# The expert layer's head, last job and tail rewritten: routing on unscaled logits, a last job of its own, returned rows summed on VectorE, a final norm per token tile

## The chip, the cores and the metric

The kernel runs on one core of a Trainium2 chip. The metric is the device time of one execution in microseconds (us), the median of several runs. The program is written instruction by instruction: each engine (PE = TensorE, ACT = ScalarE, DVE = VectorE, POOL = GpSimd, SP = SyncE) has its own list, carried out in order, and semaphores are the only coupling between lists.

## The reference, cut to what matters

Two blocks of two layers each run on 256 tokens of width 1024 in fp32. The change touches the last layer's expert feed-forward and the final norm:

```python
def rmsnorm(x, g, eps): return x * rsqrt(mean(x * x) + eps) * g
h = rmsnorm(x, ffn_norm_g[1])
logits = h @ router                          # 8 experts
top_v, top_i = lax.top_k(logits, 2)
top_w = softmax(top_v)
out = 0
for e in range(8):                           # w1, w3: 1024 x 3584, w2: 3584 x 1024
    gate_e = sum(where(top_i == e, top_w, 0))
    out = out + gate_e * ((silu(h @ w1[e]) * (h @ w3[e])) @ w2[e])
x = x + out
return rmsnorm(x, final_norm_g)
```

## The kernel before

**Weights.** Every weight passes through the core once, in chunks of 128 x 2048 fp32 (1 MB), in the order of use. SP loads them into a ring `raw` of RAW = 6 tiles and waits on `w_used` for a free one (`fetch`, L655 to L659). ACT rounds each chunk to `hi` (ring of HI = 3, `conv`, L1286 is ACT's one helper line), DVE writes the rest `lo = raw - hi` over `raw` (`conv`, L1685), and PE multiplies activations, split likewise, by both: three matmuls (hi·hi, lo·hi, hi·lo) where one fp32 product is meant, 12 of 512 columns for a chunk.

**Expert layer.** Tokens are sorted to experts on the chip. A job is one expert with up to 128 tokens; jobs 0 to 7 are the experts, and up to MORE = 3 further jobs take an expert's tokens beyond 128. In the profiled run there are 8 jobs, 0 to 7. A job has J = 14 blocks of 256 hidden units, each of three chunks: two for w1 and w3 (`up`, L1204 to L1206) and one for w2 (`down_rows`, L1185 to L1187). `job_walk` is the order that all engines share: in the turn of block j come `u0(j+1)` (first chunk of the next block), `tr(j)` (PE transposes `gprod`, ACT writes `ghi`, DVE `glo`, L2208), `u1(j+1)` (second chunk; then ACT's silu and DVE's `gprod`, L2204), and `dn(j)`. At each of the three chunk steps ACT and DVE convert the chunk two ahead. A job's `dn(13)` is done after the next job's `u0(0)`. `late` (in the turn of block 12) transposes the next job's token rows `xg` and splits them into `xhi`, `xlo`; `behind` (after `u1(0)`) evacuates the job before into `y`, and in job 0 runs DVE's `job_tables`. Ten of the blocks are two bodies in an inner hardware loop; jobs 1 to 7 are one outer hardware loop (`each_job`), with a second one under an `If` for the further jobs.

**Head.** The norm's transposed columns come as four pairs of `xhi`/`xlo` tiles. PE waits for all four, then forms the router's logits (24 matmuls, L1251 to L1253); DVE copies them (`lgT`), PE transposes, DVE multiplies by 1/rms (`lg8`), finds the two best experts, writes `chosen`; PE ranks the tokens by expert (L1263 to L1266); DVE makes the gates and then, from the rank, the one-hot `pick`. `gather` (L1153) multiplies the normalised rows `hrow` by `pick`, which gives job 0's columns. DVE goes on with the tokens' places, up to `where_i`, and splits the gathered columns (`gathered`).

**Other jobs' rows.** POOL writes the normalised rows to DRAM, fetches each next job's slots and rows (`fetch_rows`), and stores each finished job's `y` to `expert_rows` (512 KB). After the job loop it gathers, by four indirect DMAs of 512 KB, the rows that each token has in `expert_rows` (`back`), multiplies them by their shares (L2489, four of 128 x 1024), and adds them into `x` (L2492, L2493), all during job 7.

**Tail.** Job 7 fetches rows and one weight chunk for a job 8 that doesn't exist, and converts that chunk. Then PE does the last `dn(13)`, transposes `pick_g`, and four matmuls (`scatter`, L1172) return job 7's rows to their tokens; DVE adds them to `x` (L2196). The final norm squares both token tiles, takes Ln and Exp for 1/rms of both, and DVE scales (L1707); SP stores each tile.

## Time and profile before

| | |
|---|---|
| median of 3 runs | 2585.55 us (2585.35 to 2586.4) |
| the profiled execution | 2585.76 us |
| its span, first to last instruction | 2583.9 us |
| PE busy | 2509.5 us (97%) |
| DVE, ACT, POOL busy | 1818.7, 1521.9, 183.6 us |
| expert layer in the span | about 1577 to 2584 us |

A row of the timeline gives start, duration, engine, line, operation, output and inputs; a bracket holds the idle time before it and what ended it. "x8" means that many instructions in one row. PE's matmuls overlap: a 128 x 512 one is shown as 0.39 us long, yet they start every 0.23 us. The profile lists a weight load and a matmul for each; an fp32 (not rounded) matmul shows as two of each.

### The profile page before, as it was taken

The numbers are of one execution on the slowest core, as the hardware profiler recorded it, in microseconds if no ns is written. First come the engines' busy times: TensorE is split into PE (matmuls) and PEld (weight loads), VectorE is DVE, ScalarE is ACT, GpSimd is POOL, SyncE is SP. The second block draws the span as 40 slices with busy tenths as digits, with TensorE's granted clock in tenths as the row PEclk, the third lists the DMA queues.
The fourth block names the chain that finished last, engine by engine and source line by source line (L and its number), as shares of the span: only waits on it lengthen the run. The fifth ranks groups of instructions, "written<-read, shape, count | busy, mean of one in ns | idle before, by whom it ended". The sixth has DMA issues, their size and how long they took to land.

```text
span 2583.9 us, 32235 instructions
## 1 busy us (share of the span) xinstructions
PE 2509.5 (97%) x11900; PEld 2068.5 (80%) x11900; DVE 1818.7 (70%) x1795; ACT 1521.9 (59%) x1581; POOL 183.6 (7%) x141
## 2 busy tenths in 40 slices
PE   6999999999999999999999998999999999999997
PEld 5888788788878878878888876888888888888876
DVE  5577754557775555665555467888888888888887
ACT  5455544454544354545445555777777777777766
POOL 0100200010020000020000012000000000000060
PEclk8999999999999999999999999999999999999999
DMA  6444455444445564545554455999999999999995
GB/s 220 147 147 163 166 192 183 161 160 151 163 163 187 187 205 151 180 164 179 193 181 161 163 179 206 364 370 383 380 377 374 376 385 376 383 368 386 373 361 224
DMA packets 90564, 635.24 MB, mean 246 GB/s; under 512 B 10477, under 2 KB 10853, under 8 KB 15472
## 3 DMA queue, kind: packets, MB, share of 16 engines
q1 hardware_dynamic: 85104, 617.41, 65.0%
q0 software_dynamic: 4896, 16.09, 1.8%
q8 instruction: 56, 0.92, 0.1%
q10 hardware_dynamic: 480, 0.59, 0.1%
q14 instruction: 28, 0.23, 0.0%
HBM read 626.57 MB, written 7.48 MB: 245 GB/s over the span
## 4 chain that ended last, share of the span: by engine, by line
PE 88%; DVE 4%; ACT 3%; issue 3%; DMA 1%; DVEq 0%; SPq 0%; ACTq 0%
PE bank L716 13%; PE bank L718 12%; PE bank L717 12%; PE bank L1206 7%; PE bank L1204 7%; PE bank L1205 7%; PE bank L1185 4%; PE bank L1187 4%; PE bank L1186 4%; PE bank L731 3%; PE bank L733 3%; PE bank L732 3%; PE bank L705 3%; DVE w_lo L1685 2%; ACT w_hi L1286 1%
## 5 line engine op out<-in xcount | busy, mean ns | idle before, releaser
L1685 DVE TENSOR_TENSOR w_lo<-raw,w_hi 128x2048 fp32r<-128x2048 f32 x586 | 1359.2, 2322 | 492.5 <-ACT w_hi L1286 480.0
L1286 ACT ACTIVATE w_hi<-raw 128x2048 fp32r<-128x2048 f32 x586 | 1121.6, 1915 | 269.2 <-PE bank L733 102.1
L716 PE MATMUL bank<-w_hi,xhi 128*128 128x512 f32 x1456 | 580.4, 399 | 13.2 <-DVE w_lo L1685 7.5
L718 PE MATMUL bank<-w_lo,xhi 128*128 128x512 f32 x1456 | 569.7, 391 | 0.0
L717 PE MATMUL bank<-w_hi,xlo 128*128 128x512 f32 x1456 | 569.4, 391 | 0.0
L1204 PE MATMUL bank<-w_hi,xhi 128*128 128x512 f32 x896 | 359.0, 401 | 2.4 <-DVE w_lo L1685 2.4
L1206 PE MATMUL bank<-w_lo,xhi 128*128 128x512 f32 x896 | 350.2, 391 | 0.0
L1205 PE MATMUL bank<-w_hi,xlo 128*128 128x512 f32 x896 | 349.5, 390 | 0.0
L716 PEld LDWEIGHTS bank<-w_hi,xhi 128*128 128x128 f32 x1456 | 274.9, 189 | 71.8 <-issue 12.5
L718 PEld LDWEIGHTS bank<-w_lo,xhi 128*128 128x128 f32 x1456 | 274.6, 189 | 58.9
L717 PEld LDWEIGHTS bank<-w_hi,xlo 128*128 128x128 f32 x1456 | 275.2, 189 | 54.0
L1206 PEld LDWEIGHTS bank<-w_lo,xhi 128*128 128x128 f32 x896 | 168.2, 188 | 35.7
L1204 PEld LDWEIGHTS bank<-w_hi,xhi 128*128 128x128 f32 x896 | 168.3, 188 | 35.3 <-DVE w_lo L1685 3.9
L1286 ACT ACTIVATE ghi<-bank 128x256 fp32r<-128x256 f32 x178 | 64.8, 383 | 219.2 <-PE bank L705 219.2
L1205 PEld LDWEIGHTS bank<-w_hi,xlo 128*128 128x128 f32 x896 | 168.7, 188 | 31.6
L1185 PE MATMUL bank<-w_hi,ghi 128*128 128x512 f32 x448 | 176.9, 395 | 10.7 <-DVE glo L2208 10.7
L1186 PE MATMUL bank<-w_hi,glo 128*128 128x512 f32 x448 | 175.1, 391 | 0.0
L1187 PE MATMUL bank<-w_lo,ghi 128*128 128x512 f32 x448 | 175.1, 391 | 0.0
L2447 POOL TENSOR_TENSOR u<-u,gates 128x512 f32<-128x512 f32 x32 | 61.1, 1938 | 705.6 <-DVE gates L2091 705.6
L1185 PEld LDWEIGHTS bank<-w_hi,ghi 128*128 128x128 f32 x448 | 84.5, 189 | 32.5 <-DVE w_lo L1685 12.3
L731 PE MATMUL bank<-w_hi,ghi 128*128 128x512 f32 x264 | 103.0, 390 | 3.3 <-DVE glo L2152 3.3
L733 PE MATMUL bank<-w_lo,ghi 128*128 128x512 f32 x264 | 102.8, 389 | 0.0
(364 smaller groups left out, 2462.8 us busy)
## 6 DMA issues: line engine op xcount, KB each, us to landing
raw<-in_wexpert SPq DMA_DIRECT2D x337, 1024.0 KB, 5.1
raw<-in_wdense SPq DMA_DIRECT2D x249, 1024.0 KB, 4.8
expert_rows<-y POOLq DMA_DIRECT2D x7, 512.0 KB, 4.5
expert_rows<-back POOLq DMA_DIRECT2D x3, 512.0 KB, 3.8
x<-in_x SPq DMA_DIRECT2D x2, 512.0 KB, 4.9
biasT<-bias_rows POOLq DMA_DIRECT2D x1, 1024.0 KB, 6.7
normal_rows<-hrow POOLq DMA_DIRECT2D x1, 1024.0 KB, 6.3
out<-hrow SPq DMA_DIRECT2D x2, 512.0 KB, 2.7
```

The lines of the kernel that those rows point to most:

```text
L716: mm(bank[banks[t]][:, :], xhi[:, k0 + k, tok], wh, start=start and k == 0, stop=False)
L717: mm(bank[banks[t]][:, :], xlo[:, k0 + k, tok], wh, start=False, stop=False)
L718: last = mm(bank[banks[t]][:, :], xhi[:, k0 + k, tok], wl, start=False, stop=stop and k == 3)
L731: mm(b, xh, hi[:, h, o:o + 512], start=first and k == 0, stop=False)
L1185: mm(dst, ghi[:, m, 0, :], hi[:, h, w], start=first, stop=False)
L1186: mm(dst, glo[:, m, 0, :], hi[:, h, w], start=False, stop=False)
L1187: last = mm(dst, ghi[:, m, 0, :], lo[:, s, w], start=False, stop=final)
L1204: mm(bank[b][:, :], xhi[:, kt, 0:P], hi[:, h, w], start=kt == 0, stop=False)
L1205: mm(bank[b][:, :], xlo[:, kt, 0:P], hi[:, h, w], start=False, stop=False)
L1206: last = mm(bank[b][:, :], xhi[:, kt, 0:P], lo[:, s, w], start=False, stop=kt == KT - 1)
L1286: return nc.scalar.activation(dst, src, f, **kw)
L1685: V.tensor_tensor(lo[:, c % RAW, :], raw[:, c % RAW, :], hi[:, c % HI, :].bitcast(F32), ALU.subtract).then_inc(lo_ready, 1)
```

## The change

In the head the router's matmuls wait pair by pair; the experts are chosen on the logits before the 1/rms scaling, and only the difference of the two best is scaled; `rank` and `pick` come before the gates; `pick` carries 1/rms, so that `gather` reads the rows with gain alone and the normalised rows go to a tile `hnorm`; `rows_i` is written later, and half of `gathered` comes earlier. `job_tables` is split: the table for the returned rows stays, the further jobs' tables follow one by one after blocks 0 to 2 and the list after block 3. Job 0 and the last job are written out without the inner loop, and the last job is called apart from the loops. In it nothing is fetched for a next job; DVE adds the returned rows in eight 128 x 512 steps after blocks 4 to 11; `ghi`/`glo` alternate between two tiles, and the last block's transposes lie between the halves of `dn(12)`; `dn(13)` goes by output half, with `pick_g`'s transposes between. The final norm takes Square, Sqrt, a reciprocal and the scaling for each token tile, with one Sqrt ahead.

```diff
     tr(0, 0)
     u1(1, 0, 4)
     dn(0, 0, 5)
+    after(0)
+    n = 0 if first or last else (J - 3) // 2
+    if n:
+        with eng.Fori(0, n) as it:
...
     for j in range(1 + 2 * n, J - 1):
         u0(j + 1, 0, 3 + 3 * j)
         tr(j, 0)
         u1(j + 1, 0, 4 + 3 * j)
-        if j == J - 2:
+        if j == J - 2 and not last:
             late()
         dn(j, 0, 5 + 3 * j)
+        after(j)
     tr(J - 1, 0)
 def each_job(eng, job):
-    job(0, True)
+    job(0, True, False)
     eng.wait_ge(routed, 1)
     nj = eng.value_load(jobs_i[0:1, MORE + 1:MORE + 2], min_val=NE, max_val=NE + MORE)
-    with eng.Fori(1, NE) as e:
-        job(e, False)
+    end = eng.value_load(jobs_i[0:1, MORE + 2:MORE + 3], min_val=NE - 1, max_val=NE + MORE - 1)
+    with eng.Fori(1, NE - 1) as e:
+        job(e, False, False)
     with eng.If(nj > NE):
-        with eng.Fori(NE, nj) as e:
-            job(e, False)
+        with eng.Fori(NE - 1, end) as e:
+            job(e, False, False)
+    job(end, False, True)
     return nj
...
     fetch(c0 - 1, chunk(before, per - 1), nj, per)
-    fetch(c0, a["wexpert"][0, 0], nj, per)
     for t in range(NT):
-        sp.wait_ge(norm_h, NT * len([k for k in phases if k[0] == "moe"]) + t + 1)
+        sp.wait_ge(norm_h, t + 1)
         sp.dma_start(out[t * P:t * P + P, :], hrow[:, t, :]).then_inc(stored, 16)
     sp.wait_ge(stored, 16 * NT)
...
+        def turned():
+            b = X[2]
+            pe.wait_ge(pick_ready, 2)
+            pe.wait_ge(free[b], use((k, "turned"), b))
+            for t in range(NT):
+                done = tr(bank[b][:, t * P:t * P + P], pick_g[:, t, :])
+            done.then_inc(full[b], 1)
+        down_rows(k, J, J - 1, 0, 0, nj, between=turned, by_half=True)
         for b, (t, n) in zip((X[2], X[3], 2, 3), ((0, 0), (0, 1), (1, 0), (1, 1))):
             pe.wait_ge(free[b], use((k, "scatter"), b) + JU[b] * last)
+            pe.wait_ge(free[X[n]], ev((k, "D"), X[n]) + JU[X[n]] * last)
             mm(bank[b][:, :], pick_t[:, t, :], y[:, n * 512:n * 512 + 512], start=True, stop=True).then_inc(full[b], 1)
-    def down_rows(k, J, j, it, o, e, job=None):
+    def down_rows(k, J, j, it, o, e, job=None, between=lambda: None, by_half=False):
...
+        def part(m, n):
+            dst, first, final = bank[X[n]][:, :], j == 0 and m == 0, j == J - 1 and m == 1
+            w = slice(m * 1024 + n * 512, m * 1024 + n * 512 + 512)
+            mm(dst, ghi[:, m, j % 2, :], hi[:, h, w], start=first, stop=False)
+            mm(dst, glo[:, m, j % 2, :], hi[:, h, w], start=False, stop=False)
+            return mm(dst, ghi[:, m, j % 2, :], lo[:, s, w], start=False, stop=final)
+        for i in range(2):
+            for r in range(2):
+                last = part(r, i) if by_half else part(i, r)
+            if i == 0:
+                if by_half:
+                    last.then_inc(half_done, 1)
+                between()
         last.then_inc(w_used, 1)
...
         def turn(j, it):
             b = j % 2
+            if last and j == J - 1:
+                return
+            turn_block(j, it)
+        def turn_block(j, it):
+            b = j % 2
...
+            down_rows(k, J, j, it, c, e, None if j == J - 1 else e,
+                      between=(lambda: turn_block(J - 1, 0)) if last and j == J - 2 else lambda: None)
...
             b = X[0]
-            for i in range(4):
-                pe.wait_ge(free[X[i]], ev(("norm", k[1], "moe"), X[i]))
             pe.wait_ge(router_split, 1)
             for kt in range(KT):
+                if kt % 2 == 0:
+                    pe.wait_ge(free[X[kt // 2]], ev(("norm", k[1], "moe"), X[kt // 2]))
                 o = bank[b][0:NE, 0:S]
...
-    def rows_done(k, J, o, e):
-        act.wait_ge(w_used, CH[k] - 1 + o + 1 + 3 * J * e)
+    def rows_done(k, J, o, e, by_half=False):
         for n in range(2):
+            if by_half and n == 0:
+                act.wait_ge(half_done, HALF[k, "last"])
+            else:
+                act.wait_ge(w_used, CH[k] - 1 + o + 1 + 3 * J * e)
             go(y[:, n * 512:n * 512 + 512], bank[X[n]][:, :], ACT.Copy).then_inc(free[X[n]], 1)
...
             def normalised(t):
                 act.wait_ge(rows_gained, t + 1)
-                go(hrow[:, t, :], hrow[:, t, :], ACT.Copy, scale=nstat[:, 4 + t:5 + t]).then_inc(norm_h, 1)
+                go(hnorm[:, t, :], hrow[:, t, :], ACT.Copy, scale=nstat[:, 4 + t:5 + t]).then_inc(rows_normal, 1)
             normalised(0)
...
-            for t in range(NT):
-                last = go(top2[:, t, 0:1], m8[:, t, 1:2], ACT.Exp, bias=top2[:, t, 1:2])
-            last.then_inc(route_e, 1)
+            go(top2[:, :, 0:1], top2[:, :, 1:2], ACT.Exp).then_inc(route_e, 1)
             normalised(1)
             gathered(k, 0)
-            rows_done(k, FFJ["moe"], 0, nj)
-            def last_job(t):
+            rows_done(k, FFJ["moe"], 0, nj, True)
+            link(go(nstat[:, 6:7], nstat[:, 4:5], ACT.Sqrt))
+            for t in range(NT):
                 for b in ((X[2], X[3]), (2, 3))[t]:
                     act.wait_ge(free[b], ev((k, "scatter"), b) + JU[b] * (nj - 1))
-            norm(("norm", 0, None), n, None, last_job)
+                link(go(hrow[:, t, :], x[:, t, :], ACT.Square, accum_out=nstat[:, t:t + 1]))
+                go(nstat[:, 4 + t:5 + t], nstat[:, t:t + 1], ACT.Sqrt, scale=1.0 / D, bias=eps1).then_inc(root_ready, 1)
...
         if f is None:
-            dve.wait_ge(norm_rstd, n + 1)
+            moe = phases[-1][0] == "moe"
+            if not moe:
+                dve.wait_ge(norm_rstd, n + 1)
             dve.wait_ge(fgain_in, 16)
             for t in range(NT):
+                if moe:
+                    dve.wait_ge(root_ready, t + 1)
+                    link(V.reciprocal(nstat[:, 4 + t:5 + t], nstat[:, 4 + t:5 + t]))
                 V.scalar_tensor_tensor(out=hrow[:, t, :], in0=x[:, t, :], scalar=nstat[:, 4 + t:5 + t], in1=fgain[:, :],
                                        op0=ALU.mult, op1=ALU.mult).then_inc(norm_h, 1)
...
     def pick_first():
         for t in range(NT):
-            last = V.tensor_scalar(pick[:, t, :], C("slots"), jobpos[:, t, 0:1], None, ALU.is_equal)
+            last = V.tensor_scalar(pick[:, t, :], C("slots"), jobpos[:, t, 0:1], nstat[:, 4 + t:5 + t], ALU.is_equal, ALU.mult)
         last.then_inc(pick_ready, 1)
...
     def scattered(k, e):
-        dve.wait_ge(x_summed, NT)
+        dve.wait_ge(x_summed, 4 * NT)
...
+    def returned(p):
+        t, i, n = p // 4, p // 2 % 2, slice(p % 2 * 512, p % 2 * 512 + 512)
+        if p == 0:
+            dve.wait_ge(rows_back, 16 * 2 * NT)
+        dve.wait_ge(x_summed, p)
+        V.scalar_tensor_tensor(out=x[:, t, n], in0=back[i][:, t, n], scalar=share_w[:, t, i:i + 1], in1=x[:, t, n],
+                               op0=ALU.mult, op1=ALU.add).then_inc(x_summed, 1)
+    def expert_job(k, J, e, first, last):
+        def down(j, it, c):
+            if not (last and j == J - 2):
+                conv(c0 + c + 2, it, e, per)
+        def after(j):
+            if first and j < 1 + MORE:
+                if j < MORE:
+                    further_job(j)
+                else:
+                    job_list()
+            if last and 4 <= j < 4 + 4 * NT:
+                returned(j - 4)
         def up_done(j, it, c):
-            conv(c0 + c + 2, it, e, per)
+            n = c0 + c + 2
+            if last and j == J - 1:
+                dve.wait_ge(hi_ready, n + 1 + per * e)
+                halves = [(lo[:, n % RAW, w], raw[:, n % RAW, w], hi[:, n % HI, w].bitcast(F32)) for w in (slice(0, 1024), slice(1024, 2048))]
+                V.tensor_tensor(*halves[0], ALU.subtract)
+            else:
+                conv(n, it, e, per)
...
             V.tensor_tensor(gprod[:, 0, :], bank[j % 2][:, FB:2 * FB], silu[:, 0, :], ALU.mult).then_inc(free[j % 2], 1)
+            if last and j == J - 1:
+                V.tensor_tensor(*halves[1], ALU.subtract).then_inc(lo_ready, 1)
...
     def route(k):
-        V.tensor_copy(rows_i[:, :, :], C("tokens").unsqueeze(2).to_broadcast([P, NT, 16]))
...
-        dve.wait_ge(norm_rstd, len([p for p in phases if p[0] == "norm"]))
-        V.tensor_tensor(lg8[:, :, :], two(bank[b][:, 0:16]), nstat[:, 4:6].unsqueeze(2).to_broadcast([P, NT, NE]),
-                        ALU.mult).then_inc(free[b], 1)
+        V.tensor_copy(lg8[:, :, :], two(bank[b][:, 0:16])).then_inc(free[b], 1)
...
-            V.max_index(i8[:, t, :], m8[:, t, :], lg8[:, t, :])
-            last = V.tensor_scalar(top2[:, t, 1:2], m8[:, t, 0:1], -1.0, None, ALU.mult)
-        last.then_inc(route_m, 1)
-        dve.wait_ge(route_m, 1)
+            last = V.max_index(i8[:, t, :], m8[:, t, :], lg8[:, t, :])
+        link(last)
...
         last.then_inc(chosen_ready, 1)
+        dve.wait_ge(norm_rstd, len([p for p in phases if p[0] == "norm"]))
+        link(V.tensor_tensor(top2[:, :, 1:2], m8[:, :, 1:2], m8[:, :, 0:1], ALU.subtract))
+        V.tensor_tensor(top2[:, :, 1:2], top2[:, :, 1:2], nstat[:, 4:6].unsqueeze(2), ALU.mult).then_inc(route_m, 1)
+        dve.wait_ge(chosen_ready, 1)
+        b, key = X[1], (k, "rank")
+        wait_full(key, b)
+        V.tensor_copy(rank[:, :, :].rearrange("p t n -> p (t n)"), bank[b][:, 0:24]).then_inc(free[b], 1)
+        dve.wait_ge(free[b], ev(key, b))
+        link(V.scalar_tensor_tensor(out=rank[:, 0:NT, :], in0=chosen[:, :, :], scalar=1e6, in1=rank[:, 0:NT, :],
+                                    op0=ALU.mult, op1=ALU.add))
+        link(V.tensor_scalar(jobpos[:, :, 0:NE], rank[:, 0:NT, :], 1000001.0, None, ALU.subtract))
+        pick_first()
         dve.wait_ge(route_e, 1)
...
+        gathered(k, 0, (0,))
...
+        V.tensor_copy(rows_i[:, :, :], C("tokens").unsqueeze(2).to_broadcast([P, NT, 16]))
         V.tensor_copy(where_i[:, :, :], where_f[:, :, :]).then_inc(places_ready, 1)
-        gathered(k, 0)
-    def job_tables():
+        gathered(k, 0, (1,))
+    def return_tables():
...
+        V.tensor_scalar_add(jobs_f[:, MORE + 2:MORE + 3], jobs_f[:, MORE + 1:MORE + 2], -1.0)
...
-        V.tensor_copy(back_i[:, :, :], back_f[:, :, :])
-        for i in range(MORE):
+        link(V.tensor_copy(back_i[:, :, :], back_f[:, :, :]))
+    def further_job(i):
+        link(V.tensor_scalar(over[:, 3, :], over[:, 1, :], over[:, 2, i:i + 1], None, ALU.is_equal))
+        link(V.tensor_tensor(prod8[:, :, :], jobtab[:, :, 0:NE], over[:, 3, :].unsqueeze(1).to_broadcast([P, 2 * NT, NE]),
+                             ALU.mult))
...
     def expert_jobs(k):
...
-        pool.wait_ge(norm_h, NT)
-        pool.dma_start(normal_rows.rearrange("(t p) d -> p t d", p=P), hrow[:, :, :]).then_inc(normal_out, 16)
+        pool.wait_ge(rows_normal, NT)
+        pool.dma_start(normal_rows.rearrange("(t p) d -> p t d", p=P), hnorm[:, :, :]).then_inc(normal_out, 16)
...
-        def job(e, first):
+        def job(e, first, last):
             if not first:
...
                 pool.dma_start(expert_rows[bass.ds((e - 1) * P, P), :], y[:, :]).then_inc(y_out, 16)
                 pool.wait_ge(y_out, 16 * e)
-                for b in (2, 3):
-                    pool.wait_ge(full[b], fl((k, "next"), b) + JF[b] * (e - 1))
                 pool.wait_ge(pulsed, e)
-            fetch_rows(e + 1)
+            if last:
+                G.tensor_tensor(pulse[:, 1:2], pulse[:, 0:1], pulse[:, 0:1], ALU.add).then_inc(pulsed, 1)
+            else:
+                if not first:
+                    for b in (2, 3):
+                        pool.wait_ge(full[b], fl((k, "next"), b) + JF[b] * (e - 1))
+                fetch_rows(e + 1)
...
-        pool.wait_ge(rows_back, 16 * 2 * NT)
-        for t in range(NT):
-            for i in range(2):
-                last = G.tensor_scalar(back[i][:, t, :], back[i][:, t, :], share_w[:, t, i:i + 1], None, ALU.mult)
-        link(last)
-        for t in range(NT):
-            link(G.tensor_tensor(back[0][:, t, :], back[0][:, t, :], back[1][:, t, :], ALU.add))
-            G.tensor_tensor(x[:, t, :], x[:, t, :], back[0][:, t, :], ALU.add).then_inc(x_summed, 1)
```

## Rows read from the trace of the kernel before

**Rows 1.** The page's busy time of each engine.
```profile
PE 2509.5 (97%) x11900; PEld 2068.5 (80%) x11900; DVE 1818.7 (70%) x1795; ACT 1521.9 (59%) x1581; POOL 183.6 (7%) x141
```

**Rows 2.** Windows: stretch, length, busy PE, PEld, DVE, ACT, POOL; clock, DMA share, GB/s.
```profile
500.00:1000.00 500.00, 492.95 (x2436) 410.04 (x2437) 304.99 (x349) 253.60 (x307) 36.17 (x29) 1.00 0.51 172
...
1620.00:1720.00 100.00, 100.00 (x456) 82.19 (x455) 89.52 (x62) 74.79 (x62) 0.00 (x0) 1.00 0.97 370
...
2465.20:2485.30 20.10, 17.87 (x77) 13.55 (x75) 14.91 (x11) 12.84 (x11) 7.84 (x3) 1.00 1.02 422
2485.30:2525.30 40.00, 36.38 (x153) 28.97 (x153) 38.95 (x21) 24.92 (x19) 26.27 (x7) 0.96 0.86 336
```

**Rows 3.** Timeline of DVE and PE, one block of a job in the steady stretch.
```profile
1652.15 2.29 DVE L1685 TENSOR_TENSOR w_lo<-raw,w_hi 128x2048 fp32r<-128x2048 f32 x1 [0.15 <-ACT w_hi L1286]
...
1655.36 2.29 DVE L1685 TENSOR_TENSOR w_lo<-raw,w_hi 128x2048 fp32r<-128x2048 f32 x1 [0.58 <-ACT w_hi L1286]
...
1655.71 0.39 PE L1185 MATMUL bank<-w_hi,ghi 128*128 128x512 f32 x1
...
1660.59 2.29 DVE L1685 TENSOR_TENSOR w_lo<-raw,w_hi 128x2048 fp32r<-128x2048 f32 x1 [0.15 <-ACT w_hi L1286]
```

**Rows 4.** Timeline of DVE and PE in the head.
```profile
1579.72 3.23 DVE L1695 SCALAR_TENSOR_TENSOR xlo<-bank,par,xhi 128x256 fp32r<-128x256 f32 x8 [0.28 <-ACT xhi L1286]
...
1583.21 0.28 PE L1251 MATMUL bank<-xhi,router_hi 128*8 128x256 f32 x1 [2.73 <-DVE xlo L1695]
...
1587.62 0.41 DVE L2221 COPY lgT<-bank 8x256 f32<-8x256 f32 x1 [2.21 <-PE bank L1253]
...
1590.53 0.36 PE L1263 MATMUL bank<-chosen,cst 128*128 128x8 f32 x2 [2.16 <-DVE chosen L2240]
...
1592.29 0.18 DVE L2255 COPY rank<-bank 128x24 f32<-128x24 f32 x1 [0.17 <-PE bank L1266]
...
1593.51 5.94 PE L1153 MATMUL bank<-pick,hrow 128*128 128x128 f32 x32 [1.26 <-issue]
```

**Rows 5.** Waits of PE, 1577 to 1616 us: in total, times, longest.
```profile
PE bank L1185 <- DVE glo L2208: 2.8, 1, 2.8
```

**Rows 6.** Timeline of DVE in job 0, around `job_tables`.
```profile
1607.57 0.17 DVE L2297 CAST back_i<-back_f 128x4 int32<-128x4 f32 x1
...
1610.48 2.34 DVE L1685 TENSOR_TENSOR w_lo<-raw,w_hi 128x2048 fp32r<-128x2048 f32 x1
```

**Rows 7.** Timeline of PE: the first matmul of `dn(2)`, `dn(4)` and `dn(8)` in job 7.
```profile
2465.21 0.39 PE L1185 MATMUL bank<-w_hi,ghi 128*128 128x512 f32 x1
...
2485.34 0.49 PE L1185 MATMUL bank<-w_hi,ghi 128*128 128x512 f32 x1 [1.15 <-DVE glo L2208]
...
2525.30 0.39 PE L1185 MATMUL bank<-w_hi,ghi 128*128 128x512 f32 x1
```

**Rows 8.** Waits of ACT, 2465 to 2486 us.
```profile
ACT w_hi L1286 <- DMA raw<-in_wexpert: 5.4, 5, 1.9
```

**Rows 9.** Timeline of PE and DVE in the tail.
```profile
2558.93 1.03 PE L705 MATMUL bank<-ident_t,xg 128*128 128x128 f32 x8
...
2562.49 2.29 DVE L1685 TENSOR_TENSOR w_lo<-raw,w_hi 128x2048 fp32r<-128x2048 f32 x1
...
2565.24 0.49 PE L1185 MATMUL bank<-w_hi,ghi 128*128 128x512 f32 x1 [2.32 <-DVE glo L2208]
...
2569.43 3.70 PE L1172 MATMUL bank<-y,pick_t 128*128 128x512 f32 x8 [0.96 <-ACT y L1286]
...
2573.17 0.69 DVE L2196 TENSOR_TENSOR x<-bank,x 128x512 f32<-128x512 f32 x1 [0.17 <-PE bank L1172]
```

**Rows 10.** Timeline of ACT and DVE in the final norm.
```profile
2575.12 1.28 ACT L1286 ACT_TABLE_LOAD   x1
...
2578.26 2.48 DVE L1707 SCALAR_TENSOR_TENSOR hrow<-x,nstat,fgain 128x1024 f32<-128x1024 f32 x2 [4.40 <-ACT nstat L1286]
```

**Rows 11.** DMA queues, 500 to 1000 us: packets, MB, share of the 16 engines.
```profile
q8 instruction: 17, 0.28, 0.2%
```

96 lines of the change are left out of this document (35 added, 61 removed).

## The prediction

> **What bounds the kernel now.** I read the page's busy times first: PE is busy for 97% of the span [rows 1], so only time in which PE stands still, or does something that the change removes, can be won. The windows show the steady part of a job: PE has no idle time, the DMA engines are at 0.97, and DVE is busy for 89.5 of 100 us [rows 2]. One block takes 1660.59 - 1652.15 = 8.44 us, the distance between the same conversion in two blocks [rows 3]. That is 36 matmuls at one per 0.23 us and two transposes, so PE sets the pace, and DVE has 10.5% of 8.44 = 0.88 us free in a block. Three views give what is not steady: the timeline of the head [rows 4], of the first block of job 0 [rows 5, 6], of job 7 [rows 2, 7, 8], and the tail [rows 9, 10]. All edits lie there; jobs 1 to 6 keep their code but for the choice of a `ghi` tile.
>
> **The head: 3.7 us.** The router starts only when all four pairs are split, at 1583.21, and its 24 matmuls last until the copy `lgT` at 1587.62, 4.41 us [rows 4]. Waited for in pairs, six matmuls follow each pair of `xlo`; DVE makes the eight tiles in 3.23 us, 0.81 a pair, so only the last six matmuls remain after 1583.21. A quarter of 4.41 is 1.1; the first ones are faster than the mean (0.28 us long, less than half of which is their distance), so I take 0.85, and `lgT` starts at about 1584.05: 3.55 us won. If TensorE's clock falls earlier than before, they take up to 1.3 and 3.1 is won. `rows_i`'s cast and the wait for 1/rms leave the path. From `lgT` to `chosen` two of the small steps go (L2232, each under 0.15, partly overlapped): 0.15. PE's rank matmuls then take 1590.53 to 1592.29 as before, and DVE was waiting for them [rows 4], so the gates that move behind `pick` (eight small instructions) were hidden there and gain nothing by their move. Where do they go? In front of the gathered columns' split: after `pick` DVE has eight steps of the gates and nine of the shifts, at about 0.2 us each 3.4 us, against half of 5.94 us and ACT's rounding, 3.6 us, until the first half can be split; so they are covered. `gather` is 5.94 us as before. First half split, then places, then second half: PE needs the second half only after `u0(0)`, 2.8 us later. The two steps for the difference of the logits fall into DVE's wait for the rank. `gather` starts 3.55 + 0.15 = 3.7 us earlier. Bounds: 2.5 and 4.2.
>
> **Job 0: 2.8 us.** PE waits once for 2.8 us in `dn(0)` for `glo` [rows 5], because `job_tables` holds DVE until 1610.48 with the conversion behind it [rows 6]. The part that stays ends with `back_i` at 1607.74 plus one hidden addition, so the conversion starts 2.7 us earlier and `glo` as well; PE's wait goes. The other tables return as 0.7 us after each of blocks 0 to 3, below the 0.88 us free. Bounds: 2.0 and 2.8.
>
> **POOL's sums in job 7: 6.2 us.** From `dn(4)` at 2485.34 to `dn(8)` at 2525.30 four blocks took 39.96 us where 4 x 8.44 = 33.76 are due [rows 7]. In that stretch POOL is busy for 26 us (L2489 to L2493) and DVE for 38.95 of 40.0 us with only the usual work [rows 2]: DVE's conversions read two tiles in SBUF and get slower while POOL works there. DVE is what PE waits for. The sums leave POOL, so 6.2 us come back. What takes their place is eight DVE steps of 128 x 512 with a scalar and a tensor. The nearest row is the same operation at 128 x 1024, two in 2.48 us [rows 10]: 0.62 us each and a little fixed cost, 0.67. One per block, below 0.88 us. It comes right after `dn`'s conversion; the next conversion starts 0.5 us late, `glo` too, and the pause of 0.58 us before the second conversion [rows 3] takes it up. `glo` ended at 1655.36 - 0.58 = 1654.78 and PE first wanted it at 1655.71 [rows 3], so that cover holds with 0.4 us to spare; without it each step costs up to 0.67, 5.4 in all. I take 0.3 for the two tight places together (here and job 0).
>
> **The gather's traffic: 0.5 us.** Just before, from `dn(2)` to `dn(4)`, two blocks took 20.13 us instead of 16.88, 3.25 us lost [rows 7], with ACT waiting for weight chunks for 5.4 us [rows 8] and the DMA engines at 1.02 and 422 GB/s, against 370 in the steady part [rows 2]. The four gathers (2 MB) stay. What goes is the fetch of 512 KB of rows for a job that doesn't exist, and the gathers start some 6 us earlier, close behind `y`'s 512 KB. So the same 2.5 MB come in one lump rather than 3 MB with a pause. I take 0.5; bounds -0.5 and 3.2.
>
> **The tail: 8.0 us.** The eight transposes of `xg` that start at 2558.93 [rows 9] go, and `dn(12)` starts in their place. Half of it is six matmuls, 1.4 us, in which `gprod` gets ready, since DVE converts half a chunk (1.15 us) before it and not a whole one. Transposes 0.3, second half 1.4: `dn(13)` can start at 2558.93 + 3.05 = 2562.0, while `ghi` (0.4) and `glo` (0.4) are made. Before, `glo` stood behind the conversion of a chunk that nobody uses (2562.49 to 2564.78), and PE waited 2.32 us, to 2565.24 [rows 9]. That is 3.25 us. `dn(13)` with `pick_g`'s transposes lasts 2.86 + 0.3, to 2565.1, and the first half of `y` is evacuated meanwhile: the return matmuls start at 2565.15 instead of 2569.43, 4.3 us earlier [rows 9]. Their last addition starts 2573.17 - 4.3 = 2568.9 and ends at 2569.6. Then, for the second token tile: Square with its accumulator 1.2, Sqrt 0.3, reciprocal 0.2, scaling 1.24, with 0.1 for links: 2572.7. Before, the second scaling ended at 2578.26 + 2.48 = 2580.7, behind two table loads of 1.28 us and the squares and scalings of both tiles in one row [rows 10]. The store behind it is the same 512 KB. 8.0 us in all. The Sqrt ahead needs a table load and 0.3: from 2565.7 (second half of `y`) to 2567.3, in front of the first Square at 2567.9. That Square brings no load of its own is open: behind `y`'s copy it brought none. If it does, two loads more per tile, 2.6 us. Bounds of the tail: 5.4 and 8.5.
>
> The Trainium skill, "ScalarE: Activation LUTs", section "Table sets: the hidden batching unit", gives about 2.7 us for one table load. By it the Sqrt ahead would end at about 2568.7, after the first Square is due, and the tail would give an estimated 0 to 0.8 us less; this trace has 1.28 us, so I go by the row.
>
> **Code outside the loops.** The last job is reached by a branch over the unused `If` and by one more register load, where the jobs before follow each other in a loop. No row shows that branch; PE has at most about what it waited after leaving the loop at the end, 2.32 us [rows 9], and that wait has `glo` as its cause. I take 0.5, bounds 0 and 2.3. The tail is then reached without a branch, where it was hidden anyway.
>
> **Sum.** 3.7 + 2.8 + 6.2 + 0.5 + 8.0 - 0.3 - 0.5 = 20.4 us. Against the profiled execution's own 2585.76 us: 2565.4. The median of the runs is 0.2 us lower: 2565.2. I call 0.2% (5.2 us) the least that tells from no change.
>
> **The rivals.**
> - *DVE becomes the bound in job 0 and the last job.* For: only 0.2 us of its free time is left in such a block, and PE's use of `glo` is close. Against: the rows' pauses add up. If half of each inserted step shows, 8 x 0.33 + 4 x 0.35 = 4.0 us: 2569.
> - *The gather's stall goes altogether*, since the ring has recovered and less is fetched: 2.8 us more, 2562.4. Against: 422 GB/s was the ceiling, and 2 MB at it are 5 us of the weights' time.
> - *The branch to the last job is exposed on PE:* 1.8 us more than I charge, 2567. The Trainium skill, "Runtime: NRT & Kernel Launch", section "Instruction fetch mechanics", says that a taken branch whose target isn't in the fetched pages waits for a DMA of code. No run here shows it yet.
> - *Slower: the written-out jobs wait for their code.* Jobs 0 and 7 lose their inner loop, and code pages then come through DMA engines that are at 0.97. In the straight code from 500 to 1000 us 17 such pages were fetched [rows 11], one per 29 us, so two jobs of 118 us need about eight. From 20.4 / 8 = 2.6 us of PE time per page on, the change loses; at 3.5 us it gives 2593. Against: in that straight part PE was idle for only 7 us in all, under 0.5 a page, though with the DMA engines at 0.51 [rows 2].
> - *It doesn't do what it says:* if POOL's work was not what slowed DVE, but the DMA traffic, the 6.2 us stay: 2571.4. Against: DMA share is 0.86 in that stretch [rows 2].
>
> **How the numbers follow.** Forecast (2563.5 to 2567.5): 0.56. DVE the bound: 0.14. No stall: 0.10. Branch: 0.10. The sums' 6.2 us stay: 0.04. Slower: 0.03. Anything that leaves it within 0.2%: 0.03. Two in ten out leaves 2562 to 2571, which takes in the no-stall case and the upper ones but a Square load together with them. Faster by over 0.2%: 0.95, within: 0.02, slower: 0.03.
>
> **What would show it.** `gather` starts about 3.7 us earlier than 1593.51; no wait over 0.5 us at `dn(0)` of job 0; DVE's conversions stay at 2.29 us through the last job, with one step of 0.67 us per block and blocks of 8.44 us; PE waits under 0.3 us between `dn(12)` and `dn(13)`; the table load before the first Square, none after; the span ends about 11 us after `dn(13)`'s last matmul. The prediction is wrong if Squares bring loads, if blocks 4 to 11 of the last job are longer than 8.6 us, or if PE stands still for over 1 us before the last job.

## The result, and the profile after

The changed kernel takes 2569.41 us (median of 4 runs, 2568.81 to 2570.49), the kernel before 2585.86 us beside it (2585.35 to 2586.4). The ratio is 0.9938, 95% interval 0.9926 to 0.9951: 16.5 us faster. The forecast was 2565.2 us, so it is 4.2 us too low. The result lies inside the wide range (2562 to 2571) and outside the 2563.5 to 2567.5 us to which the forecast gave 0.56. The profiled execution took 2570.49 us; its span is 2568.9 us, 15.0 less than the 2583.9 of before. Where do they come from? I cut both spans at TensorE's transposes: those of the expert layer's norm, the last ones of job 6, and those of blocks 0 and 12 of the last job. The rows of this and later groups are of the timeline: start, length, engine, line, operation.

TensorE after the change, the transposes that cut the span (L708) and what the head starts:

```profile
1577.66 1.06 PE L708 MATMUL bank<-ident_t,x 128*128 128x128 f32 x8 [0.20 <-issue]
1580.22 0.28 PE L1270 MATMUL bank<-xhi,router_hi 128*8 128x256 f32 x1 [0.27 <-DVE xlo L1716]
1588.89 6.71 PE L1156 MATMUL bank<-pick,hrow 128*128 128x128 f32 x32 [1.45 <-issue]
1595.36 0.48 PE L1216 MATMUL bank<-w_hi,xhi 128*128 128x512 f32 x1
...
2427.74 0.38 PE L708 MATMUL bank<-ident_t,gprod 128*128 128x128 f32 x2
2445.90 0.38 PE L708 MATMUL bank<-ident_t,gprod 128*128 128x128 f32 x2
...
2549.38 0.38 PE L708 MATMUL bank<-ident_t,gprod 128*128 128x128 f32 x2
```

The same of the kernel before:

```profile
1578.18 1.06 PE L705 MATMUL bank<-ident_t,x 128*128 128x128 f32 x8 [0.20 <-issue]
...
2433.70 0.38 PE L705 MATMUL bank<-ident_t,gprod 128*128 128x128 f32 x2
2444.83 0.38 PE L705 MATMUL bank<-ident_t,gprod 128*128 128x128 f32 x2
...
2555.97 0.38 PE L705 MATMUL bank<-ident_t,gprod 128*128 128x128 f32 x2
```

| stretch | before | after | difference |
|---|---|---|---|
| up to the norm (code not changed) | 1578.18 | 1577.66 | -0.52 |
| norm to the end of job 6 (head, job 0) | 855.52 | 850.08 | -5.44 |
| job 6 to block 0 of the last job | 11.13 | 18.16 | **+7.03** |
| blocks 0 to 12 of the last job | 111.14 | 103.48 | -7.66 |
| from there to the end of the span | 27.93 | 19.52 | -8.41 |

Four stretches give 22.0 us, 21.5 of it in changed code, close to the forecast's 20.9 of gains, and one takes 7.0 back. That one is the surprise. What does TensorE do there? Its rows in the changed kernel, at the step from the loop over jobs to the last job:

```profile
2432.06 0.79 PE L1216 MATMUL bank<-w_hi,xhi 128*128 128x512 f32 x1 [3.94 <-issue]
...
2437.34 0.63 PE L1189 MATMUL bank<-w_hi,ghi 128*128 128x512 f32 x1
...
2438.15 0.40 PE L1191 MATMUL bank<-w_lo,ghi 128*128 128x512 f32 x1
```

The windows, among them that step, with the columns of [rows 2]:

```profile
1588.80:1596.00 7.20, 7.11 (x35) 7.06 (x36) 5.23 (x30) 1.28 (x3) 0.72 (x1) 0.57 0.96 328
1596.00:1620.00 24.00, 23.92 (x108) 19.37 (x107) 21.77 (x23) 19.74 (x16) 9.33 (x7) 1.00 0.85 324
...
2430.00:2436.00 6.00, 3.94 (x9) 3.15 (x10) 2.60 (x2) 0.83 (x1) 0.00 (x0) 0.60 0.43 169
2482.00:2550.00 68.00, 68.00 (x310) 56.09 (x309) 65.28 (x49) 50.70 (x41) 0.00 (x0) 1.00 0.93 357
```

TensorE stands still for 3.94 us, and "issue" says that no semaphore held it. Between 2430 and 2436 us the granted clock is 0.60, and the matmuls come one per 0.43 us: that is the lower level, 1.2 GHz, where 0.23 us is the upper one. The 14 from 2432.06 to 2438.15 take 6.1 us where 3.2 are due. 3.9 of pause and 2.9 of slow matmuls are 6.8 of the 7.0 us. The other windows answer to [rows 2, 5]: no wait of 2.8 us in job 0, TensorE busy without a gap in blocks 4 to 12 of the last job.

The tail after the change:

```profile
2552.34 0.39 PE L1189 MATMUL bank<-w_hi,ghi 128*128 128x512 f32 x1
...
2555.31 0.40 PE L1189 MATMUL bank<-w_hi,ghi 128*128 128x512 f32 x1
...
2558.32 3.69 PE L1177 MATMUL bank<-y,pick_t 128*128 128x512 f32 x8
...
2559.13 1.28 ACT L1305 ACT_TABLE_LOAD   x1
```

One step of the returned rows on VectorE, in block 6:

```profile
2504.32 2.29 DVE L1706 TENSOR_TENSOR w_lo<-raw,w_hi 128x2048 fp32r<-128x2048 f32 x1
2506.53 0.75 DVE L2230 SCALAR_TENSOR_TENSOR x<-back,share_w,x 128x512 f32<-128x512 f32 x1
2507.19 2.29 DVE L1706 TENSOR_TENSOR w_lo<-raw,w_hi 128x2048 fp32r<-128x2048 f32 x1
```

The step takes 0.75 us and the conversions on both sides keep their 2.29. In the tail, `dn(12)` starts at 2552.34 and `dn(13)` 2.97 us later, without the wait of [rows 9]; the returning products begin at 2558.32; the table load lies before the first Square and none follows it.

### The profile page after: what moved, and what is told of

Read it like the earlier page. It is cut to its first block, busy times and chain, and to the rows that moved or that the text cites. A ratio compares the mean times of both kernels' runs of the same rounds, so it can differ in the third digit from the quotient of the medians.

```text
span 2568.9 us, 32012 instructions
## 1 busy us (share of the span) xinstructions
PE 2509.1 (98%) x11892; PEld 2069.5 (81%) x11892; DVE 1807.3 (70%) x1804; ACT 1520.3 (59%) x1576; POOL 153.2 (6%) x131
## 4 chain that ended last, share of the span: by engine, by line
PE 91%; ACT 3%; DVE 3%; issue 2%; DMA 1%; SPq 0%; ACTq 0%; DVEq 0%
PE bank L719 13%; PE bank L721 12%; PE bank L720 12%; PE bank L1216 7%; PE bank L1218 7%; PE bank L1217 7%; PE bank L1189 4%; PE bank L1191 4%; PE bank L1190 4%; PE bank L708 3%; PE bank L734 3%; PE bank L736 3%; PE bank L735 3%; ACT w_hi L1305 1%; PE bank L1095 1%
## 5 line engine op out<-in xcount | busy, mean ns | idle before, releaser
L1706 DVE TENSOR_TENSOR w_lo<-raw,w_hi 128x2048 fp32r<-128x2048 f32 x584 | 1343.3, 2302 | 494.7 <-ACT w_hi L1305 482.5
```

Source lines behind the costliest of these rows:

```text
L1706: V.tensor_tensor(lo[:, c % RAW, :], raw[:, c % RAW, :], hi[:, c % HI, :].bitcast(F32), ALU.subtract).then_inc(lo_ready, 1)
```

## The experiments

Single times of one kernel lay up to 5.7 us apart (e3b_pool_sums), and the transposes of the norm, ahead of which no experiment changes code, start anywhere from 1576.11 (the short If) to 1579.45 us (tables in one piece) in the profiled runs. So each experiment is read twice: by its median and by a distance inside its trace. "Distance" below is that from the last transposes of the loop's last job to the first ones of the last job (11.13 before, 18.16 after). The runs of before beside them had medians of 2585.88 to 2586.06 us.

**e1_no_if and e2_one_loop: what pauses TensorE.** In `each_job`, e1 only leaves the If out; e2 makes one loop of both:

```
-            with eng.Fori(1, NE - 1) as e:
+            with eng.Fori(1, end) as e:
                 job(e, False, False)
-            with eng.If(nj > NE):
-                with eng.Fori(NE - 1, end) as e:
-                    job(e, False, False)
             job(end, False, True)
```

> The changed kernel with the unused If (the loop over further jobs) left out on TensorE, VectorE, ScalarE and GpSimd, so that the code of the last job follows the loop's end directly; the case of more than eight jobs is thereby left out. In the changed kernel 18.2 us pass on TensorE between the last transposes of the loop's last job and the first ones of the last job, where the kernel before took 11.13 us. Theory A (the branch over the If leaves the code that is fetched in sequence): the pause of 3.9 us and the slow matmuls behind it go, the distance falls to 11.5 us or less and the time to 2562.5 us (2561.5 to 2564). Rival B (any exit from the loop into code not run before waits for its fetch): the distance stays at 16 to 18 us and the time at 2569. Rival C (the low clock has another cause than the pause): the pause goes and the slow matmuls stay, 2565.

> The changed kernel with the fixed loop over jobs 1 to 6 and the If joined into one loop that ends at the register's value, so that no branch lies between it and the last job and further jobs are still served. Theory A: like the kernel without the If, 2562.5 us (2561.5 to 2564), distance from the last transposes of the loop to the first of the last job 11.5 us or less. Rival B: 2569 and 16 to 18 us. Rival D (a loop whose end is in a register costs at each turn): 0.3 us or more longer at each of the six job boundaries than the kernel without the If.

Measured: 2564.31 us (2561.62 to 2565.66), ratio 0.9914 [0.9898, 0.9931], and 2564.14 us (2562.3 to 2565.06), 0.9915 [0.9899, 0.9932]. The distance is 11.13 us in both. TensorE of the one-loop kernel at the step:

```profile
2427.64 0.38 PE L705 MATMUL bank<-ident_t,gprod 128*128 128x128 f32 x2
2427.77 0.48 PE L1213 MATMUL bank<-w_hi,xhi 128*128 128x512 f32 x1
...
2438.77 0.38 PE L705 MATMUL bank<-ident_t,gprod 128*128 128x128 f32 x2
```

The pause and the slow matmuls go together, and leaving a loop for code that was never run costs nothing by itself (B falls). C falls too: without the pause the clock keeps its upper level. A loop end in a register costs nothing against a fixed one (D falls). The medians fell by 5.1 and 5.3 us, less than the 7.0 of the distance and at the upper edge of what I gave or just beyond. The other kernels with the branch had distances of 16.27 (e3_pool_sums) and 16.21 us (e8_no_returned), so the branch costs 5 to 7 us, differently from run to run. Both of its parts are shorter in these two. TensorE stands still for 3.30 and 3.22 us, and the matmuls behind it reach the upper level after about 8, not 14. The first matmul behind the branch, in e3_pool_sums and in e8_no_returned:

```profile
2430.05 0.79 PE L1216 MATMUL bank<-w_hi,xhi 128*128 128x512 f32 x1 [3.30 <-issue]
...
2430.11 0.67 PE L1216 MATMUL bank<-w_hi,xhi 128*128 128x512 f32 x1 [3.22 <-issue]
```

So the medians, with 5.1 and 5.3 us, fit the branch as these two traces show it better than they fit the 7.0 us of the changed kernel's profiled execution, which was also the slowest of its four.

**e9_short_if: a branch, or a far branch.**

```
             with eng.If(nj > NE):
-                with eng.Fori(NE - 1, end) as e:
-                    job(e, False, False)
+                eng.value_load(jobs_i[0:1, MORE + 1:MORE + 2], ...)
```

> The changed kernel with the If still there and evaluated, but with one register load as its body in place of the loop over further jobs, which is thereby left out. Measured so far: 18.2 us between the last transposes of the loop's jobs and the first of the last job in the changed kernel, 11.13 us where no If lies between. Theory A1 (what costs is how far the branch jumps, past code that was fetched): 11.1 to 12 us here and a time within 1 us of the one-loop kernel's, 2564 us. Rival (evaluating the If and taking any branch costs): 15 to 18 us here and 2568 to 2570 us.

Measured: 2562.32 us (2561.3 to 2565.76), ratio 0.991 [0.9893, 0.9927], distance 2436.77 - 2425.63 = 11.14 us. The If and its branch cost nothing when one register load is jumped over, and 5 to 7 us when it is the code of a whole job; lengths between these two weren't run. The median is 0.8 us further off than I allowed, on the good side. Code pages fetched between 2428 and 2430 us and between 2430 and 2434 us in the changed kernel (queue: packets, MB, share):

```profile
q8 instruction: 1, 0.02, 2.9%
...
q8 instruction: 1, 0.02, 1.7%
q14 instruction: 1, 0.01, 0.5%
```

The one-loop kernel and this one have no such row between 2420 and 2440 us. The kernel before takes the same branch once, behind job 7, and two pages of the same queue come there as well. Its code pages between 2562 and 2567 us, then the windows of TensorE's pause in it and in the changed kernel:

```profile
q8 instruction: 2, 0.03, 3.0%
...
2562.92:2565.24 2.32, 0.01 (x1) 0.00 (x1) 2.32 (x3) 0.38 (x1) 0.00 (x0) 1.00 0.01 4
...
2428.12:2432.06 3.94, 0.00 (x1) 0.01 (x1) 3.38 (x3) 2.30 (x2) 0.00 (x0) 0.90 0.95 331
```

There TensorE resumes within 0.2 us of the end of `glo` (2564.69 us, 0.42 long), so the branch was over by then: it took at most 2.32 us, and the matmuls behind it came at the upper level, one per 0.23 us. The DMA engines' share was 0.01 in that pause. It was 0.95 in the pause of 3.94 us, 0.83 in that of 3.30 and 0.76 in that of 3.22. The pause is longer the busier the DMA engines are, in four traces; no run changes the traffic alone, so this cause is not shown. The Trainium skill's rule ("Runtime: NRT & Kernel Launch", "Instruction fetch mechanics"), that a taken branch to a target outside the fetched pages stalls for a DMA, agrees with all of these runs.

**e10_if_but_pe: whose code.**

```
-        def each_job(eng, job):
+        def each_job(eng, job, joined=False):
...
+            if joined:
+                with eng.Fori(1, end) as e:
+                    job(e, False, False)
+            else:
+                with eng.Fori(1, NE - 1) as e:
+                    job(e, False, False)
+                with eng.If(nj > NE):
+                    with eng.Fori(NE - 1, end) as e:
+                        job(e, False, False)
```

TensorE's call has `joined` true, the others' not.

> The changed kernel with one loop over the jobs on TensorE's own program and the loop with the If behind it on VectorE, ScalarE and GpSimd. Theory A2 (it is TensorE's own program that waits for code): the distance between those transposes falls to below 12.5 us and the time to 2564 us. Rival (the other engines' branches hold the conversions back, and TensorE would wait for them as soon as its own wait goes): a wait for w_lo or glo of 2 us or more shows on TensorE at the start of the last job, and the distance stays at 14 us or more.

Measured: 2563.53 us (2562.93 to 2564.62), ratio 0.991 [0.9894, 0.9927], distance 2439.74 - 2428.57 = 11.17 us. TensorE's own program is what waits. Between 2420 and 2440 us the rows of q8 are gone too, although the other three engines still jump, and only one page of q14 is left. The two pages of q8 come with TensorE's jump. ScalarE, which still jumps, shows a pause of its own there, and it is hidden:

```profile
2429.75 3.91 ACT L1309 ACTIVATE w_hi<-raw 128x2048 fp32r<-128x2048 f32 x2 [0.38 <-issue]
```

**e3_pool_sums and e3b_pool_sums: the sums back on GpSimd,** on the changed kernel and on the one-loop kernel.

```
-                    if last and 4 <= j < 4 + 4 * NT:
-                        returned(j - 4)
...
+                pool.wait_ge(rows_back, 16 * 2 * NT)
+                for t in range(NT):
+                    for i in range(2):
+                        last = G.tensor_scalar(back[i][:, t, :], back[i][:, t, :], share_w[:, t, i:i + 1], None, ALU.mult)
+                link(last)
+                for t in range(NT):
+                    link(G.tensor_tensor(back[0][:, t, :], back[0][:, t, :], back[1][:, t, :], ALU.add))
+                    G.tensor_tensor(x[:, t, :], x[:, t, :], back[0][:, t, :], ALU.add).then_inc(x_summed, 1)
...
+                        act.wait_ge(rows_back, 16 * 2 * NT)
```

> The changed kernel with the sums of the returned rows back on GpSimd, as in the kernel before, and none on VectorE; ScalarE waits for the returned rows before the last evacuation. Theory (VectorE's reads of two tiles slow down while GpSimd works): blocks 4 to 8 of the last job take 6 us longer in all, conversions there 3 to 4 us instead of 2.29, time 2575.5 us (2574.5 to 2577). Rival (it was the traffic, which stays as it is here): blocks stay at 8.41 us, time 2569.

> The one-loop kernel with the sums of the returned rows on GpSimd, none on VectorE. On the changed kernel this edit gave 13.44 us for block 5, 9.42 for block 6 and 6.2 us in all, but only 3.9 us in the medians, with the branch's pause differing by 1.9 us between the profiled runs. Theory (the sums cost 6 us and the medians differ by the pause's and the start's variation): 6 us more than the one-loop kernel, 2570 us (2569 to 2571.5). Rival (the profile exaggerates, 3.9 us is the true price): 2568 us.

Measured: 2573.26 us (2572.15 to 2574.79), ratio 0.9953 [0.9936, 0.9969], 3.9 over the changed kernel; and 2572.28 us (2568.12 to 2573.83), 0.9942 [0.9925, 0.9958], 8.1 over the one-loop kernel. The medians miss both of my figures, one on each side; their mean is 6.0. The traces agree with each other. Transposes of blocks 4, 5, 6, 7 and 8 in e3b_pool_sums, and its VectorE meanwhile:

```profile
2476.94 0.38 PE L705 MATMUL bank<-ident_t,gprod 128*128 128x128 f32 x2
2485.49 0.38 PE L705 MATMUL bank<-ident_t,gprod 128*128 128x128 f32 x2
2498.54 0.38 PE L705 MATMUL bank<-ident_t,gprod 128*128 128x128 f32 x2
2508.38 0.38 PE L705 MATMUL bank<-ident_t,gprod 128*128 128x128 f32 x2
2516.80 0.38 PE L705 MATMUL bank<-ident_t,gprod 128*128 128x128 f32 x2
```

```profile
2482.62 8.59 DVE L1704 TENSOR_TENSOR w_lo<-raw,w_hi 128x2048 fp32r<-128x2048 f32 x2
...
2491.46 4.14 DVE L1704 TENSOR_TENSOR w_lo<-raw,w_hi 128x2048 fp32r<-128x2048 f32 x1
```

Four blocks take 39.86 us, where the changed kernel takes 33.63 (from 2482.13 to 2515.76): 6.2 us, the term of the forecast. In e3_pool_sums they take 2518.41 - 2478.55 = 39.86 as well. Two conversions of the fence take 4.3 us each and one 4.14, instead of 2.29, at a DMA share of 0.75 from 2484 to 2508 us. In the changed kernel the share is 1.00 in blocks 4 to 8 and they keep 2.29. So it isn't the traffic.

Which part of GpSimd's work does it? GpSimd multiplies until 2481.96 us and then adds, in four steps until 2497.88. From e3b_pool_sums, the multiplications, two conversions beside them, and the first addition:

```profile
2466.40 15.56 POOL L2550 TENSOR_SCALAR back<-back,share_w 128x1024 f32<-128x1024 f32 x4 [11.68 <-DMA back<-expert_rows,back_i]
...
2474.24 5.07 DVE L1704 TENSOR_TENSOR w_lo<-raw,w_hi 128x2048 fp32r<-128x2048 f32 x2
...
2482.04 2.59 POOL L2553 TENSOR_TENSOR back<-back,back 128x1024 f32<-128x1024 f32 x1
```

Beside the multiplications, which read one tile, a conversion takes 2.3 to 2.9 us; beside the additions, which read two, 4.1 to 4.3. Most of the price is that of the additions. No run moves only one of the two.

The cut at block 4 hides a part. The multiplications begin before it, and blocks 2 to 8 as a whole take 2516.80 - 2457.39 = 59.41 us in e3b_pool_sums against 52.06 in the one-loop kernel, 7.35 us more; for e3_pool_sums against the changed kernel it is 58.36 against 52.44, 5.92 us more. This is one reason why the medians lie so far apart.

**e8_no_returned: the gathers' traffic.** The four indirect gathers, `returned` and the wait for it are left out.

> The changed kernel without the four gathers of the returned rows and without their sums, so the output leaves out what jobs 0 to 6 return. Theory (their 2 MB beside the weights' stream cost the one long block, 10.39 us instead of 8.41): all blocks of the last job take 8.41 us and the time falls by 2.0 us, to 2567.4 us. Rival (the stream is behind already, since the stretch of 18 us at the job's start moved only 227 GB/s and the fetch of rows follows): the long block stays, 2569. If the VectorE steps cost something too, which the blocks of 8.40 to 8.42 us say they don't, the time falls by more than 2.5 us.

Measured: 2567.16 us (2564.66 to 2569.15), ratio 0.993 [0.9913, 0.9947], 2.25 us below the changed kernel. The median can't be put down to the gathers alone, because the branch's distance also differs between the two traces (16.21 and 18.16 us). The blocks can be compared. Blocks 2 to 4 take 2476.93 - 2460.12 = 16.81 us there; in the changed kernel the block from 2471.74 to 2482.13 alone is 2.0 us too long. Blocks 4 to 8 take 33.63 us in both, so VectorE's eight steps cost nothing. The output of this run leaves out what jobs 0 to 6 return.

**e11_spread: the same gathers, apart.** On the one-loop kernel:

```
+                        if g:
+                            pool.wait_ge(rows_back, 16 * g)
+                            pool.wait_ge(lo_ready, CH[k] + 6 + 6 * g + 3 * FFJ["moe"] * (nj - 1))
+                            G.tensor_tensor(pulse[:, 2:3], pulse[:, 0:1], pulse[:, 0:1], ALU.add).then_inc(paced, 1)
+                            pool.wait_ge(paced, g)
...
-                if p == 0:
-                    dve.wait_ge(rows_back, 16 * 2 * NT)
+                if p % 2 == 0:
+                    dve.wait_ge(rows_back, 16 * (p // 2 + 1))
```

> The one-loop kernel with the four gathers of the returned rows issued apart: each waits for the one before and for a weight chunk two blocks further on, and each VectorE step pair waits for its own gather. Measured so far: one long block, 10.2 us for 8.41, in the one-loop kernel and none without the gathers. Theory (2 MB in one lump hold the weights' stream up for longer than it is ahead; 0.5 MB at a time it can bear): the long block goes, 1.7 us less than the one-loop kernel's 2564.1 us: 2562.4 us. Rival (the stream has no slack at all at a DMA share of 0.97 in the steady part, so each gather of 1.25 us at 420 GB/s shows later as a wait of TensorE): four blocks longer by 0.4 us or more each, time 2564 us or more.

Measured: 2561.44 us (2560.76 to 2562.18), ratio 0.9903 [0.9887, 0.992], 2.7 us below the one-loop kernel and 8.0 below the changed one: the fastest of all. Its transposes of blocks 2, 3 and 4:

```profile
2455.62 0.38 PE L705 MATMUL bank<-ident_t,gprod 128*128 128x128 f32 x2
2464.02 0.38 PE L705 MATMUL bank<-ident_t,gprod 128*128 128x128 f32 x2
2472.44 0.38 PE L705 MATMUL bank<-ident_t,gprod 128*128 128x128 f32 x2
```

From block 2 on each block is 8.40 to 8.42 us long. In the trace, blocks 2 to 8 take 50.44 us against 52.06 in the one-loop kernel, 1.6 us less, as expected; the other 1.1 us of the median's 2.7 isn't accounted for. The bytes are the same; what cost time was that they came in one lump.

**e4b_tables_once: job 0's tables in one piece again,** on the one-loop kernel: `return_tables` calls `further_job` for all i and `job_list`, `after` does neither.

> The one-loop kernel with all of the job tables made in one piece behind block 0's columns in job 0, as in the kernel before. My steps: TensorE waits again for glo in dn(0), about 2.7 us, and 2564.1 becomes 2566.8 us; VectorE no longer has a table step behind blocks 0 to 3, which won't show, since the windows there have TensorE busy for 99.7 of 100 us. Rival (the split pieces cost as much in job 0 as the wait did): no difference, 2564 us.

Measured: 2567.96 us (2564.35 to 2568.6), ratio 0.9924 [0.9907, 0.994], 3.8 more. `glo` of block 0 comes 1610.60 - 1579.45 = 31.15 us after the norm's transposes, in the one-loop kernel 1606.14 - 1577.67 = 28.47: 2.7 us, as forecast. From the norm's transposes to the end of job 6 the difference is 852.33 - 849.97 = 2.4 us, so the split pieces cost 0.3. The median moved by 1.4 us more than this distance; the norm starts 1.8 us later in this trace than in the one-loop kernel's, in code that is the same.

**e5b_four_pairs: the router waits for all pairs again,** on the one-loop kernel.

```
-                    for kt in range(KT):
-                        if kt % 2 == 0:
-                            pe.wait_ge(free[X[kt // 2]], ...)
+                    for i in range(4):
+                        pe.wait_ge(free[X[i]], ...)
+                    for kt in range(KT):
```

> The one-loop kernel with the router waiting for all four pairs of split columns again. Its 24 matmuls now end 3.2 us after the first pair's wait; behind the last pair they took 4.41 us in the kernel before. My steps: lgT comes 2.9 to 3.6 us later with respect to the start of the norm, and the gather 5.94 instead of 6.7 us long, as before: 2.2 to 3.6 us more, 2567 us. Rival (the gather's lower clock takes back all that the pairs win): under 1 us more, 2564.5 us.

Measured: 2566.09 us (2564.91 to 2567.74), ratio 0.9923 [0.9907, 0.994], 2.0 more. Its rows on TensorE:

```profile
1576.16 1.07 PE L705 MATMUL bank<-ident_t,x 128*128 128x128 f32 x8 [0.20 <-issue]
...
1581.07 0.28 PE L1267 MATMUL bank<-xhi,router_hi 128*8 128x256 f32 x1 [2.62 <-DVE xlo L1713]
...
1586.90 0.57 PE L1279 MATMUL bank<-chosen,cst 128*128 128x8 f32 x2 [2.07 <-DVE chosen L2287]
...
1590.62 6.62 PE L1153 MATMUL bank<-pick,hrow 128*128 128x128 f32 x32 [1.45 <-issue]
1597.00 0.48 PE L1213 MATMUL bank<-w_hi,xhi 128*128 128x512 f32 x1
```

The gather starts 14.46 us after the norm's transposes; in the one-loop kernel it starts at 1588.88, 11.21 after them. That is 3.25 us, and 3.2 remain at the first expert matmul (20.84 against 1595.30 - 1577.67 = 17.63). So the pairs are nearly all of the head's gain at the first expert matmul (3.3 us). The time moved, though: here `lgT` (1584.08) is only 2.2 us later relative to the norm, since the router's matmuls ran at the full clock, and the rank matmuls got the low one (0.57 us long, where the one-loop kernel's first two are 0.36).

**e6c_tail_whole: the order in the tail,** on the one-loop kernel: the last transposes stand behind a whole `dn(12)`, `down_rows(k, J, J - 1, 0, 0, nj)` without `by_half`, then `turned()`, and `rows_done` without `by_half`.

> The one-loop kernel with dn(12) and dn(13) of the last job each whole: the last gprod's transposes stand behind dn(12), pick_g's behind dn(13), and y is evacuated after dn(13). The transposes of rows for no further job and the spare conversion stay away. In the changed kernel 8.94 us pass from the last job's second last transposes (block 12) to the first product that returns rows. My steps: dn(13) waits about 1.3 us for ghi and glo, and the first half of y is evacuated 0.6 us later in the chain: 10.7 to 11.3 us, and 2 us more in all, 2566 us. Rival (the order is worth the full 3.25 us of my step on dn(12)): 12.2 us or more, 2567.4 us. Rival (worth nothing, since the removed conversion alone freed glo): 8.9 to 9.3 us, 2564 us.

Measured: 2566.45 us (2564.87 to 2567.81), ratio 0.9924 [0.9908, 0.9941], 2.3 more. Its rows:

```profile
2548.45 0.49 PE L1187 MATMUL bank<-w_hi,ghi 128*128 128x512 f32 x1 [1.02 <-DVE glo L2260]
...
2552.30 3.69 PE L1175 MATMUL bank<-y,pick_t 128*128 128x512 f32 x8 [0.59 <-DVE pick_t L2202]
```

The returning products start 10.92 us after block 12's transposes (2541.38), not 8.94: 2.0 us, of which 1.02 is the wait for `glo`.

**e7b_no_early_sqrt: the table load,** on the one-loop kernel: the line with `ACT.Sqrt` on `nstat[:, 6:7]` goes.

> The one-loop kernel without the Sqrt on one column ahead of the first Square. Squares bring no table load and the first Sqrt does: my step is that the load of 1.28 us then stands between the first Square and its Sqrt, where the early one took place while ScalarE had nothing to do, so everything behind comes 1.3 us later, less the 0.2 us of the early Sqrt's spare time: 1.3 us more, 2565.4 us by the profile's distances (the median's own variation is 2 us). Rival (VectorE sets the end, and the later root is hidden behind the additions): under 0.3 us more.

Measured: 2564.94 us (2564.53 to 2566.49), ratio 0.9919 [0.9902, 0.9935], 0.8 more. ScalarE:

```profile
2553.73 1.06 ACT L1302 ACTIVATE hrow<-x 128x1024 f32<-128x1024 f32 x1 [2.00 <-DVE x L2218]
...
2554.89 1.28 ACT L1302 ACT_TABLE_LOAD   x1
2556.19 0.29 ACT L1302 ACTIVATE nstat<-nstat,epst 128x1 f32<-128x1 f32 x1
```

The first Square brings no load, the first Sqrt does. From block 12's transposes to the end of the span it is 2562.9 - 2542.00 = 20.9 us against 2561.7 - 2541.86 = 19.8: 1.1 us. Where the tail's code is the same, that distance is 19.46 to 19.85 us long from kernel to kernel, so the load is worth 1.0 to 1.4.

## Why the prediction was right, and where it was not

- **Code outside the loops: the step that failed.** I charged 0.5 us for the branch, with 2.3 as the upper bound, taken from TensorE's 2.32 us wait for `glo` at the end of the kernel before. That wait does hold the same branch, and bounds it there, with the DMA engines idle (share 0.01); at the new place, in the middle of the weights' stream, the bound doesn't hold. The branch costs 7.0 us in the profiled run and 5.1 to 5.3 in the medians. The rival "the branch to the last job is exposed on PE" was the right one and priced too low as well. Two things were missing: the pause itself, 3.9 us, and that TensorE comes back from it at the lower clock, 2.9 us more. The prediction's own sign of being wrong, TensorE standing still for over 1 us before the last job, came true. With 7.0 in place of 0.5 my sum would have been 2571.7, 2.3 above what was measured.
- **The number is partly luck.** The missing 6.5 us of the branch were made up for in part: the changed stretches gained 0.6 us more than forecast, unchanged code 0.5, and the profiled execution lay 1.1 us above the median where I had reckoned with 0.2. The time alone would have spoken for the rival "DVE becomes the bound" (2569). The trace refutes it: from block 4 on the blocks stay at 8.40 to 8.42 us.
- **The head.** 3.7 forecast; the first expert matmul is 1599.20 - 1595.36 = 3.84 us earlier in the span, 0.52 of it from ahead of the change: 3.3. The gather did start about as early as forecast (4.62 us, 4.10 without the 0.52), but lasts 6.71 us, not 5.94 [rows 4], at a granted clock of 0.57.
- **Job 0.** 2.8 and the 0.3 for tight places: right (2.7, and 0.3 to 0.6 given back).
- **The sums.** 6.2 was right for the blocks from `dn(4)` to `dn(8)`, and that GpSimd's work is the cause is shown by both experiments. Over blocks 2 to 8 they put it at 5.9 and 7.4 us. A step takes 0.75 us, not 0.67, and is hidden.
- **The gather's traffic.** 0.5 forecast, 1.3 measured from `dn(2)` to `dn(4)`: 3.25 us lost before, 2.0 now, 0 when the gathers are spread. This split rests on where one cuts. GpSimd's multiplications began at 2480.26 us in the kernel before, 5 us ahead of its `dn(4)`, so a part of the 3.25 was theirs; cut at the transposes, the same blocks lose 1.3 us and the next four 8.3. What doesn't depend on the cut is the sum of both terms: 60.1 us from `dn(2)` to `dn(8)` before, 52.4 after, 7.7 gained where 6.7 were forecast.
- **The tail.** 8.0 forecast, 8.4 measured. 2.0 of it are the order, 1.1 the early table load. The other 5.3 (the transposes and the conversion that went, the norm by token tile) weren't taken apart.
- **"The written-out jobs wait for their code"** didn't come true: TensorE is busy for 68.00 of 68 us in blocks 4 to 12 of the last job and for 119.42 of 120 us in job 0 (1610 to 1730 us). What waits is the jump, not the straight code.

Open is why the branch's pause is 3.94 us in one run and 3.2 to 3.3 in two others (the DMA share beside it is the one difference found), and what turns the clock down in the head now in one place and now in another.

## What to carry to other kernels

A branch over a long unused body on the engine that sets the pace costs microseconds: put the rare case in the same loop (a loop end in a register was free here), or keep what is jumped over short. A bound read from a row holds for the traffic and the place in which the row was taken: the same branch took at most 2.32 us at a DMA share of 0.01 and 3.94 us at 0.95. Where a cost moves to another place, a cheap edit that avoids it is worth more than a better guess. If GpSimd must do elementwise work beside VectorE's two-tile subtractions, look at how many tiles its steps read: in these traces multiplications of one tile cost a conversion at most 0.6 us, additions of two about 2. And a transfer that doesn't fit beside a stream may fit in quarters.
